# Two gated feed-forwards cut in parts of 6, 8 and 8 tiles, and wave tables made in the layers

## The chip, the cores and the metric

The kernel runs on one core of a Trainium2 chip. The metric is the device time of one execution in microseconds; lower is better. Five engines work side by side, each through its own list of instructions in order: TensorE (PE) multiplies, VectorE (DVE), ScalarE (ACT) and GpSimd (POOL) do elementwise work, and SyncE (SP) mostly issues transfers. They wait for each other by semaphores.

## The reference, cut to what matters

```python
D_MODEL, SEQ, DEPTH, D_FF_2 = 1024, 512, 2, 2816

def first_block(x, ...):                     # two layers
    for l in range(DEPTH):                   # attention, convolution, retention, and then
        ...                                  # x + rms_norm(square(relu(rms_norm(x) @ w_up)) @ w_down)

def swiglu_ffn(x, w_in, w_down):             # w_in 1024 x 5632, w_down 2816 x 1024
    a, b = jnp.split(x @ w_in, 2, axis=-1)
    return (jax.nn.silu(a) * b) @ w_down

def hybrid_layer_2(x, mem, ...):             # the third part
    x = x + 0.5 * swiglu_ffn(rmsnorm(x, ffn1_norm), ffn1_w_in, ffn1_w_down)
    u = rmsnorm(x, mix_norm)
    ...       # a scan with cos and sin of (a_im * dt) * t, attention, memory attention, w_out
    x = x + 0.5 * swiglu_ffn(rmsnorm(x, ffn2_norm), ffn2_w_in, ffn2_w_down)
    return x
```

`mem` (256 x 1024) is normalised too and multiplied by `w_kv` right after the first feed-forward. All of it is float32.

## The kernel before

Activations stand with features on the 128 partitions and the 512 tokens along a row, so 1024 features are 8 tiles. A float32 product is made of three matmuls of a faster type: each operand is split in a rounded part (`_hi`) and the rest (`_lo`), and hi*hi, hi*lo and lo*hi are added in PSUM. `product` does this for a block of weights of up to 1024 rows and 256 columns: 2 output tiles x 8 x 3 = 48 matmuls of 512 tokens. The weights come in blocks into `w_raw` (two slots). ScalarE copies a block to `w_hi` (`round_block`), VectorE subtracts to get `w_lo` (`rest_block`), both two blocks ahead of TensorE; SyncE issues the next load when the slot is free.

**Quarter products.** `seven` does a block of 1024 x 256 weights by Strassen's scheme: tokens, weight rows and weight columns are cut in halves, and seven products of quarters (each 4 x 3 matmuls of 256 tokens) take the place of eight. The price is on the other engines. `seven_sums` and `last_sum` make four sums of weight quarters, `pair_round` and `pair_rest` split the seven weight terms in four steps, and `one_product`, `two_products`, `three_products`, `last_late`, `last_early` and `first_late` put the outputs together from the four banks. The fifth product adds to the bank of the first, so TensorE waits until `one_product` (ScalarE, to `two_sum`) has copied it; the sixth waits for `three_products`. Before the first quarter product of a feed-forward `whole_scaled` (VectorE) makes the normalised activations `h_whole`, `direct_round` and `direct_rest` split them, `token_sums` (GpSimd) forms the sums of token halves in place, and `sums_round` (ScalarE) and `sums_rest` (VectorE) split these to `t_hi` and `t_lo`. TensorE waits on `whole` for all of it.

**The two layers.** A layer's feed-forward has four parts of 4 up blocks and 4 down blocks. The up blocks of part 0 are direct, those of parts 1 to 3 are quarter products. The code calls the four down blocks of a part `downs`, and `begun` is the first quarter block of the next part, whose weights are prepared beside the last two down blocks.

**The third part.** The second feed-forward (`ffn2`) is cut in parts of 8, 8 and 6 of its 22 tiles: up blocks of the part, then its four down blocks, which VectorE adds to `x_sb` with factor 0.5. Part 0 is direct and parts 1 and 2 (14 pairs of an `a` and a `b` tile) are quarter products. The first feed-forward (`ffn1`) is direct throughout: 11 turns of two up blocks, `g_hi` and `g_lo` with all 22 tiles, and then 16 down blocks (6, 6, 5 and 5 tiles for each of 4 output pairs), which add up in PSUM.

Beside these 16 blocks of `ffn1` stand two pieces of other work. One is the norm of `mem`. The other is the wave tables, cos and sin of the scan's phases, 16 of them, each 128 x 2 x 512: `whole_turns` (GpSimd, 2 instructions), `phase_step` (VectorE, 3), `waves` (ScalarE, 3), and a store to `trig_kept` in DRAM issued by SyncE. The buffer `made` holds three of them.

The order of all this is written out by hand, engine by engine: `layer_scalar`, `layer_vector` and `layer_gpsimd` for the layers, `third_scalar` and its like for the third part.

## Time and profile before

| | us |
|---|---|
| median of 3 runs | 2402.59 |
| lowest, highest | 2402.18, 2402.71 |
| the profiled execution | 2402.1 |
| its span in the trace | 2400.3 |
| TensorE busy | 2385.4 |
| VectorE busy | 1591.3 |
| ScalarE busy | 1094.6 |
| GpSimd busy | 344.6 |

The span goes from the first to the last instruction of the trace; 1.8 us of the execution's time lie around it. Busy times are sums of the instructions' times with overlaps counted once. A matmul's printed duration reaches beyond the start of the next one, so TensorE's pace is read from starts. A row in time order gives the start, the duration, the engine, the line of the kernel, the operation and `out<-in`; what stands in brackets is the idle time before it and who ended it.

### The profile page before, as it was taken

What the parts mean: (1) busy time and instruction counts of PE and PEld (TensorE: products, weight loads), DVE (VectorE), ACT (ScalarE), POOL (GpSimd) and SP (SyncE); (2) the same over time, 40 slices, a digit from 0 to 9 for tenths busy, and PEclk for the clock granted to TensorE, in tenths of its full rate; (3) what the DMA queues carried; (4) which work ended last, traced back from release to release, by engine and by line L of the source; (5) the groups of instructions that cost most, each with busy time, mean ns of one, the idle gap of its engine ahead of it and who ended that gap; (6) DMA issues with size and microseconds to landing.
All of it is one profiled execution on the core that took longest, in us unless ns stands there. A gap on an engine that the chain in (4) does not pass through costs nothing.

```text
span 2400.3 us, 33986 instructions
## 1 busy us (share of the span) xinstructions
PE 2385.4 (99%) x13482; PEld 2014.5 (84%) x13482; DVE 1591.3 (66%) x2231; ACT 1094.6 (46%) x1626; POOL 344.6 (14%) x259
## 2 busy tenths in 40 slices
PE   9999999999999999999999999999999999999998
PEld 7877998998886989889988888877778788889997
DVE  7775775665977567557644347769995386359685
ACT  5346553555445546336522236522335564335444
POOL 1231030001132121001111124300000121120001
PEclk9999999999999999999999999999999999999999
DMA  4312222323230222223232225643442143222322
GB/s 169 145 45 88 89 87 90 123 88 106 101 128 18 106 90 104 88 106 109 86 105 89 103 102 183 221 148 119 145 158 80 49 169 134 88 106 82 114 87 88
DMA packets 46849, 260.13 MB, mean 108 GB/s; under 512 B 5424, under 2 KB 7984, under 8 KB 22768
## 3 DMA queue, kind: packets, MB, share of 16 engines
q1 hardware_dynamic: 44448, 249.07, 29.6%
q0 software_dynamic: 640, 5.51, 0.6%
q10 hardware_dynamic: 1616, 3.54, 0.5%
q8 instruction: 101, 1.65, 0.3%
q14 instruction: 44, 0.36, 0.1%
HBM read 240.27 MB, written 16.78 MB: 107 GB/s over the span
## 4 chain that ended last, share of the span: by engine, by line
PE 91%; DVE 5%; ACT 2%; issue 2%; DMA 0%; DVEq 0%; SPq 0%; ACTq 0%
PE gemm L487 60%; PE gemm L1104 5%; PE gemm L1105 5%; PE gemm L1106 5%; PE gemm L780 1%; PE gemm L791 1%; PE gemm L782 1%; DVE w_lo L437 1%; DVE out_sb L1912 1%; PE turned L1418 1%; PE mixed L1432 1%; PE score L1409 1%; PE gemm L520 1%; PE gemm L673 1%; PE gemm L674 1%
## 5 line engine op out<-in xcount | busy, mean ns | idle before, releaser
L437 DVE TENSOR_TENSOR w_lo<-w_raw,w_hi 128x2048 fp32r<-128x2048 f32 (+4 forms) x157 | 341.9, 2177 | 204.9 <-ACT w_hi L429 204.8
L487 PE MATMUL gemm<-h_hi,w_hi 128*128 128x512 f32 x1136 | 454.2, 400 | 1.0 <-DVE w_lo L437 1.0
L487 PE MATMUL gemm<-h_hi,w_lo 128*128 128x512 f32 x1136 | 443.3, 390 | 0.0
L487 PE MATMUL gemm<-h_lo,w_hi 128*128 128x512 f32 x1136 | 442.7, 390 | 0.0
L429 ACT ACTIVATE w_hi<-w_raw 128x2048 fp32r<-128x2048 f32 (+4 forms) x167 | 292.9, 1754 | 202.9 <-PE gemm L487 169.0
L487 PEld LDWEIGHTS gemm<-h_hi,w_hi 128*128 128x128 f32 x1136 | 213.6, 188 | 55.5 <-issue 8.3
L487 PEld LDWEIGHTS gemm<-h_hi,w_lo 128*128 128x128 f32 x1136 | 213.2, 188 | 45.5
L487 PEld LDWEIGHTS gemm<-h_lo,w_hi 128*128 128x128 f32 x1136 | 213.6, 188 | 42.2 <-issue 1.0
L487 PE MATMUL gemm<-f_hi,w_hi 128*128 128x512 f32 x480 | 187.2, 390 | 0.7
L487 PE MATMUL gemm<-f_hi,w_lo 128*128 128x512 f32 x480 | 186.8, 389 | 0.0
L487 PE MATMUL gemm<-f_lo,w_hi 128*128 128x512 f32 x480 | 186.8, 389 | 0.0
L1104 PE MATMUL gemm<-t_hi,w_hi 128*128 128x256 f32 x608 | 172.3, 283 | 0.0
L1105 PE MATMUL gemm<-t_lo,w_hi 128*128 128x256 f32 x608 | 172.0, 283 | 0.0
L1106 PE MATMUL gemm<-t_hi,w_lo 128*128 128x256 f32 x608 | 172.0, 283 | 0.0
L1042 ACT ACTIVATE w_hi<-w_raw 128x1024 fp32r<-128x1024 f32 x76 | 80.5, 1059 | 169.7 <-DVE w_raw L1021 98.7
L487 PE MATMUL gemm<-g_hi,w_hi 128*128 128x512 f32 x340 | 132.5, 390 | 0.0
L487 PE MATMUL gemm<-g_lo,w_hi 128*128 128x512 f32 x340 | 132.3, 389 | 0.0
L487 PE MATMUL gemm<-g_hi,w_lo 128*128 128x512 f32 x340 | 132.3, 389 | 0.0
L1105 PE MATMUL gemm<-h_lo,w_hi 128*128 128x256 f32 x456 | 129.0, 283 | 0.0
L1106 PE MATMUL gemm<-h_hi,w_lo 128*128 128x256 f32 x456 | 129.0, 283 | 0.0
L1104 PE MATMUL gemm<-h_hi,w_hi 128*128 128x256 f32 x456 | 129.0, 283 | 0.0
L1051 DVE TENSOR_TENSOR w_lo<-w_raw,w_hi 128x1024 fp32r<-128x1024 f32 x76 | 93.9, 1236 | 37.5 <-ACT w_hi L1042 37.0
(549 smaller groups left out, 5315.9 us busy)
## 6 DMA issues: line engine op xcount, KB each, us to landing
w_raw<-in_w SPq DMA_DIRECT2D x179, 1024.0 KB, 4.8
w_raw<-in_w SPq DMA_DIRECT2D x12, 768.0 KB, 4.2
w_raw<-in_w SPq DMA_DIRECT2D x17, 512.0 KB, 3.8
trig_kept<-made SPq DMA_DIRECT2D x16, 512.0 KB, 5.9
trig<-trig_kept SPq DMA_DIRECT2D x16, 512.0 KB, 6.5
w_raw<-in_w SPq DMA_DIRECT2D x8, 640.0 KB, 4.5
bias_t<-in_att_bias SPq DMA_DIRECT2D x2, 1536.0 KB, 9.1
decay_t<-in_c_decay SPq DMA_DIRECT2D x2, 1536.0 KB, 8.0
```

The lines of the kernel that those rows point to most:

```text
L429: act.activation(flat(w_hi, b), flat(w_raw, b), ACT.Copy).then_inc(S["w_rounded"], 1)
L437: dve.tensor_tensor(flat(w_lo, b), flat(w_raw, b), flat(w_hi, b).bitcast(F32), ALU.subtract).then_inc(S["w_rest"], 1)
L487: mm = pe.matmul(dst, lhs, rhs, start=b.first and k == 0 and j == 0, stop=b.last and k == b.kt - 1 and j == 2)
L520: pe.matmul(dst, wh[:, k, c], hi[:, k, :], start=k == 0, stop=False)
L673: pe.matmul(dst, wh[:, k, c], h_hi[:, k, :], start=k == 0, stop=False)
L674: pe.matmul(dst, wl[:, k, c], h_hi[:, k, :], start=False, stop=False)
L780: pe.matmul(dst, wh[:, k, c], h_hi[:, k, TOKENS[e]], start=k == 0 and m == 0, stop=False, skip_group_check=True)
L1042: act.activation(pair_of(w_hi, b, q), pair_source(b, q), ACT.Copy).then_inc(S["term_hi"] if q < 3 else S["w_rounded"], 1)
L1051: dve.tensor_tensor(pair_of(w_lo, b, q), pair_source(b, q), pair_of(w_hi, b, q).bitcast(F32), ALU.subtract).then_inc(S["term_lo"] if q < 3 ...
L1104: pe.matmul(dst, wh[:, c], h, start=q < 4 and k == 0, stop=False, skip_group_check=q >= 4)
L1105: pe.matmul(dst, wh[:, c], r, start=False, stop=False, skip_group_check=q >= 4)
L1106: mm = pe.matmul(dst, wl[:, c], h, start=False, stop=k == 3, skip_group_check=q >= 4)
```

## The change

Both feed-forwards of the third part go through one function for each engine, with parts of 6, 8 and 8 tiles. Part 0 is direct, and the other 16 pairs are quarter products: 16 more in `ffn1` and 2 more in `ffn2`. The loops of `ffn1` are written out. The norm of `mem` moves into part 1 of `ffn1`, beside its down blocks.

The wave tables are made in the two layers. Each down block of parts 1 and 2 of a layer gets one wave, at its end in the code, so a layer makes 8 and both make 16. `made` holds one wave now, so `whole_turns` of a wave waits for the store of the wave before. The store is issued by ScalarE, right after the wave; after the fourth wave of a part `log_and_exp` loads ScalarE's table for the rest of the layer.

```diff
-FFN_PARTS = (6, 6, 5, 5)
-GATED_PARTS = (8, 8, 6)
+GATED_PARTS = (6, 8, 8)
...
-    ffn("ffn1")
+    def gated(name):
+        for part, tiles in enumerate(GATED_PARTS):
+            start[f"{name}_up{part}"] = len(out)
+            at = sum(GATED_PARTS[:part])
+            if part:
+                for t in range(at, at + tiles):
+                    out.append(Piece(0, t * P, WCOLS, KD, "seven", name + "_in"))
+            else:
...
+            for j in range(DM // WCOLS):
+                out.append(Piece(at * P, j * WCOLS, WCOLS, tiles, "feat", name + "_down"))
+
+    gated("ffn1")
...
             token_sums(pool, cnt)
             for part in range(1, PARTS):
-                for b in plan1[UP[part]:UP[part] + 4]:
+                for b in plan1[UP[part] + (part > 1):UP[part] + 4]:
                     last_sum(pool, b)
+                if part == 1:
+                    pool.wait_ge(S["units"], plan1[DOWN[1]].u0)
+                    pool.dma_start(time_t[:], A["c_time"]).then_inc(S["time_in"], 16)
...
+                if part < PARTS - 1:
+                    for j in range(4):
+                        whole_turns(pool, wave_at(lay, part, j))
+                        if j == 2:
+                            last_sum(pool, plan1[UP[part + 1]])
...
                     else:
                         for q in range(2) if j == 2 else range(2, 4):
                             pair_round(act, begun, q)
...
+                    if part:
+                        waves(act, wave_at(lay, part, j))
+                        if j == 3:
+                            log_and_exp(act)
...
                     else:
                         for q in range(2, 4):
                             pair_rest(dve, begun, q)
+                    if (lay, part, j) == (0, 0, 1):
+                        steps_and_turns(dve, step)
+                    if part:
+                        phases(dve, wave_at(lay, part, j))
...
-        made = at("made", [P, 3, 2, SEQ], F32, 66)
+        time_t = at("time_t", [P, SEQ], F32, FZ + 72)
+        made = at("made", [P, 2, SEQ], F32, FZ + 74)
...
+        def whole_turns(pool, s):
+
+            if s:
+                pool.wait_ge(*wave_stored(s - 1))
+            to = made[:, 0, :]
...
+        def waves(act, s):
+
+            act.wait_ge(S["phased"], s + 1)
...
+            act.dma_start(trig_kept[s], made[:]).then_inc(S[f"trig_moved{s % 3}"], 16)
...
+            for part in range(len(GATED_PARTS)):
+                if part:
+                    seven_part("ffn1", part)
+                ups, downs = gated_blocks("ffn1", part)
+                for j, b in enumerate(downs):
+                    def mem_total(m):
+                        if (part, j, m) == (1, 1, 1):
+                            pe.wait_ge(S["sq_added"], added_by(MEM_NORM))
...
+                    if (part, j) == (1, 1):
+                        mem_squares_added()
+                    if (part, j) == (1, 2):
+                        mem_scaled()
+                    down_rests("ffn1", part, j)
```

**ScalarE at the end of a layer's down blocks, part 1.** First before the change, from the weights of `begun` to `one_product` (`two_sum`) and on:

```order
L1042 ACTIVATE w_hi<-w_raw 128x1024 [waits w_in1,units]
L1042 ACTIVATE w_hi<-w_sums 128x512 [waits last_summed,units]
L1180 ACTIVATE two_sum<-gemm 128x256 [waits term_read]
L1042 ACTIVATE w_hi<-w_raw 128x1024 [waits w_summed,term_read]
L1042 ACTIVATE w_hi<-w_sums 128x1024 [waits w_summed,term_read]
```

The same place after the change:

```order
L1036 ACTIVATE w_hi<-w_raw 128x1024 [waits w_in1,units]
L1036 ACTIVATE w_hi<-w_sums 128x512 [waits last_summed,units]
L2355 ACTIVATE made<-made 128x512 [waits phased]
L2357 ACTIVATE made<-made 128x512 [waits trig_s]
L2358 ACTIVATE made<-made,quarter 128x512
L2360 DMA trig_kept<-made 128x1024 [waits trig_s]
L570 ACT_TABLE_LOAD
L1174 ACTIVATE two_sum<-gemm 128x256 [waits term_read]
L1036 ACTIVATE w_hi<-w_raw 128x1024 [waits w_summed,term_read]
L1036 ACTIVATE w_hi<-w_sums 128x1024 [waits w_summed,term_read]
```

The fourth wave, its store and a table load now stand between the weights of `begun` and the copy of its first product.

**VectorE at the same place.** Before, from the adding of the last two down blocks to `three_products`:

```order
L1051 TENSOR_TENSOR w_lo<-w_raw,w_hi 128x1024 [waits term_hi]
L1051 TENSOR_TENSOR w_lo<-w_sums,w_hi 128x1024 [waits term_hi]
L2109 TENSOR_TENSOR out_sb<-out_sb,gemm 128x512 [waits units,g_free]
L2109 TENSOR_TENSOR out_sb<-out_sb,gemm 128x512 [waits units]
L1051 TENSOR_TENSOR w_lo<-w_raw,w_hi 128x1024 [waits term_hi]
L1051 TENSOR_TENSOR w_lo<-w_sums,w_hi 128x512 [waits w_rounded]
L1118 TENSOR_TENSOR two_sum<-two_sum,gemm 128x256 [waits first_out,term_read]
L1018 TENSOR_TENSOR w_sums<-w_raw 128x512 [waits term_lo,w_in0]
```

After:

```order
L2386 SCALAR_TENSOR_TENSOR made<-time_t,state_par,made 128x512 [waits turns_s]
L2389 SCALAR_TENSOR_TENSOR made<-time_t,state_par,made 128x512 [waits fract]
L2392 TENSOR_SCALAR made<-made 128x512 [waits fract_low]
L2123 TENSOR_TENSOR out_sb<-out_sb,gemm 128x512 [waits units,g_free]
L2123 TENSOR_TENSOR out_sb<-out_sb,gemm 128x512 [waits units]
L1045 TENSOR_TENSOR w_lo<-w_raw,w_hi 128x1024 [waits term_hi]
L1045 TENSOR_TENSOR w_lo<-w_sums,w_hi 128x512 [waits w_rounded]
L2386 SCALAR_TENSOR_TENSOR made<-time_t,state_par,made 128x512 [waits turns_s]
L2389 SCALAR_TENSOR_TENSOR made<-time_t,state_par,made 128x512 [waits fract]
L2392 TENSOR_SCALAR made<-made 128x512 [waits fract_low]
L1112 TENSOR_TENSOR two_sum<-two_sum,gemm 128x256 [waits first_out,term_read]
L1012 TENSOR_TENSOR w_sums<-w_raw 128x512 [waits term_lo,w_in0]
```

The third wave stands ahead of the last two additions and the fourth ahead of `two_products`; each waits for GpSimd (`turns_s`).

**VectorE beside the down blocks of part 0 in `ffn2`.** Before:

```order
L1192 TENSOR_TENSOR h_lo<-h_whole,h_hi 128x2048 [waits more_hi]
L3731 SCALAR_TENSOR_TENSOR x_sb<-gemm,x_sb 128x512 [waits units] x2
L437 TENSOR_TENSOR w_lo<-w_raw,w_hi 128x2048 [waits w_rounded]
L3731 SCALAR_TENSOR_TENSOR x_sb<-gemm,x_sb 128x512 [waits units] x2
L437 TENSOR_TENSOR w_lo<-w_raw,w_hi 128x2048 [waits w_rounded]
L1198 TENSOR_TENSOR t_lo<-h_whole,t_hi 128x2048 [waits more_hi] x2
L3731 SCALAR_TENSOR_TENSOR x_sb<-gemm,x_sb 128x512 [waits units] x2
```

After:

```order
L1186 TENSOR_TENSOR h_lo<-h_whole,h_hi 128x2048 [waits more_hi]
L3367 SCALAR_TENSOR_TENSOR x_sb<-gemm,x_sb 128x512 [waits units] x2
L427 TENSOR_TENSOR w_lo<-w_raw,w_hi 128x1536 [waits w_rounded]
L3367 SCALAR_TENSOR_TENSOR x_sb<-gemm,x_sb 128x512 [waits units] x2
L427 TENSOR_TENSOR w_lo<-w_raw,w_hi 128x1536 [waits w_rounded]
L1192 TENSOR_TENSOR t_lo<-h_whole,t_hi 128x2048 [waits more_hi] x2
L3367 SCALAR_TENSOR_TENSOR x_sb<-gemm,x_sb 128x512 [waits units] x2
```

Nothing moved; the down blocks' weights are 6 tiles instead of 8. `ffn1` now has the same rows.

## Rows read from the trace of the kernel before

**Rows 1.** the page: TensorE (PE) busy, and its granted clock
```profile
PE 2385.4 (99%) x13482; PEld 2014.5 (84%) x13482; DVE 1591.3 (66%) x2231; ACT 1094.6 (46%) x1626; POOL 344.6 (14%) x259
...
PEclk9999999999999999999999999999999999999999
```

**Rows 2.** the waits of TensorE, whole span: total us, times, longest
```profile
PE mixed L725 <- DVE sq_f L917: 1.6, 2, 0.8
PE turned L1248 <- DVE rs L1359: 1.5, 1, 1.5
```

**Rows 3.** TensorE in time order: start us, duration, engine, line, operation
```profile
2128.43 0.39 PE L487 MATMUL gemm<-g_hi,w_hi 128*128 128x512 f32 x1
...
2171.95 0.28 PE L1104 MATMUL gemm<-h_hi,w_hi 128*128 128x256 f32 x1
```

**Rows 4.** busy time by window: eight pairs by quarter products, VectorE as DVE
```profile
2172.00:2252.00 80.00, 80.00 (x669) 80.00 (x668) 74.15 (x114) 44.47 (x63) 0.00 (x0) 1.00 0.30 107
```

**Rows 5.** VectorE, GpSimd, ScalarE before the first quarter products, in time order
```profile
2134.04 5.38 DVE L1184 SCALAR_TENSOR_TENSOR h_whole<-x_sb,par_sb,rs 128x512 f32<-128x512 f32 x8
...
2143.79 13.70 POOL L1152 TENSOR_TENSOR h_whole<-h_whole 128x1024 f32<-128x1024 f32 x4 [23.30 <-DVE h_lo L1192]
...
2157.52 3.72 ACT L1173 ACTIVATE t_hi<-h_whole 128x2048 fp32r<-128x2048 f32 x2 [5.14 <-POOL h_whole L1152]
...
2159.47 4.50 DVE L1198 TENSOR_TENSOR t_lo<-h_whole,t_hi 128x2048 fp32r<-128x2048 f32 x2 [4.24 <-ACT t_hi L1173]
...
2165.08 0.69 DVE L1018 TENSOR_TENSOR w_sums<-w_raw 128x512 f32<-128x512 f32 x1
...
2168.28 1.23 DVE L1051 TENSOR_TENSOR w_lo<-w_raw,w_hi 128x1024 fp32r<-128x1024 f32 x1 [0.46 <-ACT w_hi L1042]
...
1442.91 1.76 DVE L437 TENSOR_TENSOR w_lo<-w_raw,w_hi 128x1536 fp32r<-128x1536 f32 x1
```

**Rows 6.** the first layer, end of its second down projection, in time order
```profile
416.14 0.28 PE L1104 MATMUL gemm<-h_hi,w_hi 128*128 128x256 f32 x1
...
421.89 0.28 PE L1104 MATMUL gemm<-h_hi,w_hi 128*128 128x256 f32 x1
...
385.71 2.29 DVE L437 TENSOR_TENSOR w_lo<-w_raw,w_hi 128x2048 fp32r<-128x2048 f32 x1 [1.32 <-ACT w_hi L429]
...
410.46 1.21 DVE L1051 TENSOR_TENSOR w_lo<-w_sums,w_hi 128x1024 fp32r<-128x1024 f32 x1
...
418.58 0.69 DVE L1051 TENSOR_TENSOR w_lo<-w_sums,w_hi 128x512 fp32r<-128x512 f32 x1
...
421.48 0.41 DVE L1125 TENSOR_TENSOR three_sum<-two_sum,gemm 128x256 f32<-128x256 f32 x1
...
417.83 0.36 ACT L1180 ACTIVATE two_sum<-gemm 128x256 f32<-128x256 f32 x1
```

**Rows 7.** one wave in time order (POOL, DVE, ACT), and a table load
```profile
1469.82 0.70 POOL L2773 TENSOR_SCALAR made<-time_t,state_par 128x512 f32<-128x512 f32 x1 [3.60 <-DMA trig_kept<-made]
...
1472.13 0.75 DVE L3292 SCALAR_TENSOR_TENSOR made<-time_t,state_par,made 128x512 f32<-128x512 f32 x1 [2.21 <-POOL made L2776]
...
1474.17 0.63 ACT L2860 ACTIVATE made<-made 128x512 f32<-128x512 f32 x1 [1.37 <-DVE made L3301]
...
1475.37 0.71 ACT L2863 ACTIVATE made<-made,quarter 128x512 f32<-128x512 f32 x1
...
1430.19 1.28 ACT L2928 ACT_TABLE_LOAD   x1
```

**Rows 8.** the stores of the waves, issue to landing; transfers at 404 to 412
```profile
DMA to landing us min/median/max: 2.6/5.9/7.4
...
404.00:412.00 8.00, 8.00 (x37) 6.64 (x36) 5.32 (x7) 2.01 (x2) 1.29 (x1) 1.00 0.00 0
```

**Rows 9.** squares of the memory and their addition, in time order
```profile
1420.33 2.55 ACT L536 ACTIVATE mem_t<-mem_sb 128x256 f32<-128x256 f32 x8
...
1424.11 2.32 DVE L3355 TENSOR_TENSOR mem_t<-mem_t 128x1024 f32<-128x1024 f32 x2
```

More of the change, by code:

```diff
@@ L254, in third_pieces @@
         out.append(Piece(0, c, WCOLS, KD, "feat", "w_out2"))
[L255 to L267 removed]
+    gated("ffn2")
     return out, start
@@ L2368, in third_sync @@
         def third_sync(sp):
[L2369 to L2375 removed]
+            for b in plan2[0:AT2["u"]]:
                 load_block(sp, b)
[L2377 to L2379 removed]
             def load_trig(s):
@@ new lines, in third_tensor @@
+            opening_in_halves(pe, ups[:2], 2 * DEPTH - 1, sq_f)
+            for n, b in enumerate(ups[2:]):
+                product(pe, b, h_hi, h_lo, each=None if n else second_total(pe, 2 * DEPTH - 1, sq_f))
+            for part in range(len(GATED_PARTS)):
[6 more added lines that the diff above has]
+                            pe.wait_ge(S["sq_added"], added_by(MEM_NORM))
+                            pe.matmul(o_ps[:, 0:MEM], ones[:], mem_sq[:, 0, :], start=True,
+                                      stop=True).then_inc(S["norm_sum"], 1)
+                    product(pe, b, g2_hi, g2_lo, tile_ready=None if j else (S["g2_s"], sum(GATED_PARTS[:part])),
+                            halfway=mem_total)
@@ new lines, in seven_part @@
+            def seven_part(name, part):
+                ups, downs = gated_blocks(name, part)
+                for u, b in enumerate(ups):
+                    if u:
+                        pair_round(act, b, 3)
+                    one_product(act, b)
+                    if u:
+                        gated_round(ups[u - 1], u - 1)
+                    for q in range(3):
+                        if q == 2:
+                            gate_kept(b)
+                        if not b.closes:
+                            pair_round(act, plan[b.n + 1], q)
+                        elif q < 2:
+                            begun_round(act, downs[0], q)
+                    gate_silu(b)
+                gated_round(ups[-1], len(ups) - 1)
+                round_block(act, downs[1].n)
@@ new lines, in down_rounds @@
+            def down_rounds(name, part, j):
+                ups, downs = gated_blocks(name, part)
+                if part == 0 and j == 0:
+                    direct_round(act, gated_counts(name), ups[-1])
+                if part == 0 and j == 2:
+                    sums_round(act, gated_counts(name))
+                if j < 2 or part == LAST_PART:
+                    round_block(act, downs[j].n + 2)
+                else:
+                    begun = gated_blocks(name, part + 1)[0][0]
+                    for q in range(2) if j == 2 else range(2, 4):
+                        pair_round(act, begun, q)
@@ L2945, in third_scalar @@
+            norm_squares(act, x_sb, x2_sq, wait=(S["g_free"], downs[0].t0), tiles=(KD - 2, KD - 1))
             norm_rooted(act, N0 + 2)
@@ L3238, in third_scalar @@
+                if part < LAST_PART:
+                    for j, b in enumerate(downs):
+                        down_rounds("ffn2", part, j)
             log_and_exp(act)
```

702 lines of the change are left out of this document (289 added, 413 removed).

## The prediction

> **What bounds the kernel now.** I read four views in this order. The page says how full TensorE is: it is busy for 99% of the span, and its granted clock never shows less than 9 tenths [rows 1]. The waits of TensorE say that nothing stands in front of it: no wait of the whole span is over 1.5 us [rows 2], and in a stretch of quarter products TensorE is busy 80 of 80 us [rows 4]. So matmuls taken out shorten the span one for one, and any wait that is put in front of TensorE lengthens it one for one. The order in time then gives TensorE's pace, and the last view is the same stretch on the other engines, to see how close they run behind it.
>
> Pace. In the second feed-forward of the third part, the down products of part 0 (4 blocks of 48 matmuls, 192 in all) start at 2128.43 and the first quarter product starts at 2171.95 [rows 3]: 43.52 us / 192 = 0.2267 us for a matmul of 512 columns. In the quarter products 669 matmuls of 256 columns take 80.00 us [rows 4]: 0.120 us each. The durations printed for one matmul overlap and are not used.
>
> **What the matmuls save.** A direct pair of tiles is 2 tiles x 8 x 3 = 48 matmuls: 48 x 0.2267 = 10.88 us. A pair by quarter products is 7 x 4 x 3 = 84: 84 x 0.120 = 10.08 us. The gain is 0.80 us a pair. The first feed-forward changes 16 pairs, the second 2 more than before (14 to 16): 18 x 0.80 = 14.4 us. The down products keep their matmuls (22 x 8 x 3 in either cut). In the steady part of the eight pairs VectorE is busy 74.15 of 80 us [rows 4], and TensorE has no wait. The first feed-forward runs the same instructions on each engine, so I cost its steady part at nothing; the cover is those 6 us, 0.7 us a pair.
>
> The Trainium skill (TensorE: Matmul & The Clock Gate, Part 1) gives start-to-start as N / 2.4 GHz plus 2.5 ns. An estimate from that page is 215.8 and 109.2 ns, 1.19 us a pair and 21 us in all. The rows disagree with it for these matmuls, more so at 256 columns, and the measurement decides.
>
> **Entry to the quarter products: part 0 has 6 tiles in place of 8.** Before the first quarter product, the whole normalised activations have to be made, summed by GpSimd, rounded by ScalarE and subtracted by VectorE. This chain starts when the last up product ends and is covered by the down products of part 0. Counted from 2128.43 [rows 3, 5]: VectorE starts h_whole at +5.6, GpSimd's sums run from +15.4 to +29.1 (13.70 us), ScalarE rounds t_hi from +29.1, VectorE's t_lo runs +31.0 to +35.5, the weight sums start at +36.7, and the first w_lo of the quarter products ends at 2169.51, +41.1. The down products end at +43.5: 2.4 us to spare. After the change the down products are 144 matmuls, 144 x 0.2267 = 32.6 us. The chain keeps every step. Only the weights ahead of it are smaller: VectorE's 128x1536 takes 1.76 us where 128x2048 takes 2.29 [rows 5, 6], and ScalarE's copy ahead of it shrinks in a like share, by my estimate 0.4 us. So w_lo is ready at +40.2 and TensorE waits 7.6 us. Bounds: 5 us (a chain shorter by the 2.3 us that t_lo's second half takes, if less traffic speeds the shared engines) and 8.5 us (no shortening). I take 7.6, since every row of the chain is this kernel's. Both feed-forwards enter this way: 2 x 7.6 = 15.2 us, of which nothing was paid before.
>
> **The waves in the layers.** Each layer has two down stretches (its parts 1 and 2) of four blocks of 10.9 us, and each block now gets one wave: GpSimd 2 instructions, VectorE 3, ScalarE 3 and a store issued by ScalarE. One buffer holds the wave, so GpSimd may begin wave s only when the store of wave s-1 has landed. Costs by the old waves [rows 7]: GpSimd 1469.82 to 1472.13, 2.3 us; VectorE to 1474.17, 2.0; ScalarE to 1476.08, 1.9. The store took 2.6 to 7.4 us, median 5.9, there in competition with weight loads; here the queues are idle (share 0.00 from 404 to 412 [rows 8]), so I take 3.0 with its issue. For the first three waves of a stretch VectorE and ScalarE have idle time, and their place is late in the block, so they are hidden. The fourth is not. Follow the first layer [rows 6]: VectorE ends the second w_lo at 411.67, and wave 2 is next: VectorE 413.6, ScalarE 415.6, store landed 418.6, GpSimd 420.9 for wave 3, VectorE 422.9, ScalarE 424.9, issue of the store and then a table load of 1.28 [rows 7]: 426.4. Only then, in ScalarE's order, comes the copy two_sum, 0.36 us: 426.8. It started at 417.83 before. TensorE's fifth quarter product adds to the bank that this copy reads, and started at 421.89. It now waits 5.0 us. VectorE then has the addition after the copy, three weight sums and three_sum, whose end the sixth product wants: about 2.75 us after the copy (421.48 + 0.41 minus the end of the weights at 419.2), against 1.44 us of the fifth product, so 1.3 us more. The next block starts with VectorE about a microsecond later than usual, and I add 0.1. The sum is 6.4 us a stretch, 4 stretches: 25.6 us. Queued behind VectorE's wait for wave 3 are exactly those additions; behind ScalarE's, the copy and the next weights' rounding; behind GpSimd's, one weight sum. Bounds: if wave 3's turns are ready when VectorE gets there (419.3), the copy ends at 424.8 and the loss is 4.2 us. With stores of 5.9 us each, waves 1 and 2 slip too, the copy ends near 431.7, and the loss is 11.4 us. I take 6.4, as the store's row is nearest the short end when nothing competes.
>
> In the first feed-forward the 16 waves go away from VectorE, ScalarE, GpSimd and SyncE's queue, which also loses 16 stores and their waits. They lay beside matmuls there and TensorE had no wait, so this gains nothing. GpSimd's one weight sum a stretch that now stands behind wave 2 ends near 415.3, ahead of ScalarE's use of it at 417.3.
>
> **The memory's norm.** It now stands in part 1 of the first feed-forward. ScalarE has, after block 0 (10.9 us), the weight copy (about 1.9), a table load 1.28 and eight squares 2.55 [rows 7, 9]; VectorE adds them in 2.32 and about 0.7: 20.2 us after the start of the down products. TensorE wants the sum halfway through the second tile of block 1: 16.3 + 2.7 = 19.0. I cost it at 1.1 us, between 0 and 2.
>
> **Sum.** -14.4 + 15.2 + 25.6 + 1.1 = +27.5 us. The profiled run took 2402.1 us, 0.5 below the median of 2402.59, so I add the sum to the median: 2430 us.
>
> **Rivals.** Chances are at the end of each.
> (1) The forecast, all four terms: 2430 us. 0.40.
> (2) The same waits, and the clock falls in them. No row shows TensorE idle for more than 1.5 us [rows 2] and the clock is full throughout [rows 1], so a pause of 5 to 8 us is new here. If the first two quarter products after an entry (24 x 0.120 = 2.9 us) ran at half pace, 2.9 us more twice, and about 0.6 in each layer stretch, where half is hidden by the wait for three_sum: 8 us, 2438. The Trainium skill (TensorE: Matmul & The Clock Gate, Part 1) says that an idle array drops to half clock and recovers with activity; no row here shows it. 0.22.
> (3) Stores at their old median: 25.6 becomes 45.6, 2450 us. Against it is the idle share [rows 8]. 0.06.
> (4) Only the entries wait, since the layers' waves finish in time: 2404.5 us. It needs a chain 5 us shorter than the rows. 0.09.
> (5) Only the layers wait: 2415 us. 0.10.
> (6) The other side: cover holds, and TensorE is never last in any of the six places. The one mechanism is that GpSimd, whose steps head both chains, runs faster beside a less busy VectorE. It decides from a mean wait of 2.4 us at each of six places (14.4 / 6). All waits gone gives 2388 us. For it: old GpSimd steps overlapped VectorE's. Against: GpSimd is 13.7 of 41 us at the entry and 2.3 of 15 in the layers; it would have to be twice as fast, and the order in ScalarE's queue stays. 0.13.
>
> **How the numbers follow.** The likeliest is 2430. About 0.2% (5 us) is what a measurement of this kernel tells from no change. Faster: case 6, 0.13. Same: case 4, 0.09, and a little of 5: 0.10. Slower: the rest, 0.77. The range leaves out case 6 and most of case 3: 2404 to 2446. It takes in the entry waits at 5 to 8.5, the layers at 4.2 up to 9, and the clock.
>
> **What would show it.** In the waits of TensorE: two of 7 to 8 us for VectorE's w_lo at the entries of the feed-forwards, four of about 5 us in the layers for ScalarE's two_sum, each followed by about 1.3 us for three_sum, and one of a microsecond for the memory's sum. The steady quarter products of the first feed-forward should keep 0.120 us. The granted clock after the waits decides case 2. If the fourth wave's VectorE steps stand ahead of 419 us in the first layer, my store or GpSimd price is wrong; if t_lo ends before +30, the entry is.

## The result: slower by 2.0%, and by 20 us more than forecast

| | before | after |
|---|---|---|
| median, us | 2402.39 (4 runs) | 2449.85 (4 runs) |
| lowest, highest | 2402.05, 2402.71 | 2448.48, 2450.84 |
| ratio, 95% interval | | 1.0197 (1.0183 to 1.0210) |
| span of the profiled execution | 2400.3 | 2449.0 |
| TensorE's mean granted clock | 0.999 | 0.989 |

The kernel lost 47.5 us where 27.5 was forecast, outside the range of 2404 to 2446. These are the waits of TensorE after the change; before it, no wait was over 1.5 us [rows 2]. Columns: who waited for whom, us in total, times, longest.

```profile
PE gemm L1098 <- ACT two_sum L1174: 25.3, 4, 6.6
PE gemm L1098 <- issue: 8.1, 2, 4.0
PE mixed L554 <- DVE x_sq L623: 4.8, 1, 4.8
PE gemm L477 <- DVE w_lo L427: 4.7, 4, 2.0
```

Row 1 is the four layer stretches (a stretch is the four quarter blocks behind a part's down blocks) and row 2 the two entries. Row 3 is the end of `ffn1`. Row 4 is mostly the down blocks of part 0 in both feed-forwards, 1.98 and 1.97 us. The forecast had no wait over a microsecond in the places of rows 3 and 4.

**The first of the four stretches, in the first layer.** This is the place of [rows 6], in time order on VectorE, ScalarE, GpSimd and TensorE. Waves are numbered from 0 within a part, so wave 3 is the fourth. L2386 to L2392 are VectorE's steps of a wave, L2355 to L2358 ScalarE's, L2335 and L2338 GpSimd's.

```profile
412.69 0.74 DVE L2386 SCALAR_TENSOR_TENSOR made<-time_t,state_par,made 128x512 f32<-128x512 f32 x1
...
422.17 0.75 DVE L2386 SCALAR_TENSOR_TENSOR made<-time_t,state_par,made 128x512 f32<-128x512 f32 x1 [2.17 <-POOL made L2338]
```
```profile
416.65 0.33 ACTq L2360 DMA_DIRECT2D trig_kept<-made  x1
...
424.21 0.63 ACT L2355 ACTIVATE made<-made 128x512 f32<-128x512 f32 x1 [5.55 <-DVE made L2392]
...
426.50 1.28 ACT L570 ACT_TABLE_LOAD   x1 [0.39 <-ACT made L2358]
427.79 0.38 ACT L1174 ACTIVATE two_sum<-gemm 128x256 f32<-128x256 f32 x1
```
```profile
419.32 1.24 POOL L2335 TENSOR_SCALAR made<-time_t,state_par 128x512 f32<-128x512 f32 x1 [8.77 <-DMA trig_kept<-made]
420.65 1.49 POOL L2338 TENSOR_SCALAR made<-made 128x512 f32<-128x512 f32 x1
```
```profile
428.32 0.55 PE L1098 MATMUL gemm<-h_hi,w_hi 128*128 128x256 f32 x1 [5.59 <-ACT two_sum L1174]
```

Wave 2 starts on VectorE at 412.69, its store is issued at 416.65 and landed at 419.3, GpSimd ends wave 3's turns at 422.1, and the copy `two_sum`, which stood at 417.83 before [rows 6], starts at 427.79. TensorE idles 5.59 us.

**The clock after it.** The same stretch in windows. A row gives the window, its length, the busy time (and the number of instructions) of PE, PEld, DVE, ACT and POOL, then PEclk, the granted clock, and the share and GB/s of the transfers.

```profile
422.40:428.40 6.00, 0.41 (x4) 0.24 (x3) 1.83 (x4) 3.54 (x5) 0.00 (x0) 0.93 0.53 220
428.40:434.00 5.60, 5.60 (x26) 5.51 (x27) 5.14 (x8) 2.29 (x4) 1.28 (x1) 0.50 0.00 0
434.00:436.00 2.00, 2.00 (x17) 2.00 (x17) 1.47 (x3) 1.97 (x3) 0.00 (x0) 0.89 0.00 0
```

From 427.6, still within the wait, the granted clock is 0.50, the 1.2 GHz level, until about 434.4. Matmuls of 256 columns start 0.213 us apart there, and 0.120 us apart before and after.

**An entry**, in `ffn1`. The down products of part 0 start at 1273.65; two waits of TensorE follow, with VectorE's first `w_lo` of them, its `t_lo`, and GpSimd's sums:

```profile
1292.11 0.50 PE L477 MATMUL gemm<-g_hi,w_hi 128*128 128x512 f32 x1 [1.98 <-DVE w_lo L427]
...
1312.76 0.55 PE L1098 MATMUL gemm<-h_hi,w_hi 128*128 128x256 f32 x1 [4.03 <-issue]
```
```profile
1289.08 2.98 DVE L427 TENSOR_TENSOR w_lo<-w_raw,w_hi 128x1536 fp32r<-128x1536 f32 x1
...
1302.63 4.49 DVE L1192 TENSOR_TENSOR t_lo<-h_whole,t_hi 128x2048 fp32r<-128x2048 f32 x2 [6.71 <-ACT t_hi L1167]
```
```profile
1288.04 12.61 POOL L1146 TENSOR_TENSOR h_whole<-h_whole 128x1024 f32<-128x1024 f32 x4 [22.34 <-DVE h_lo L1186]
```

The view names no engine for the second wait (`issue`). The first `w_lo` of quarters ends at 1312.65, 0.11 us ahead of the matmul, so I put the wait down to it. That is +39.0 on the forecast's scale (+40.2 there, +41.1 before). The six-tile down products take 1312.76 - 1273.65 = 39.11 us in place of 144 x 0.2267 = 32.65: 6.46 of wait, 1.98 of it in the middle and 4.03 at the end. Behind the second the clock is down again:

```profile
1309.00:1313.00 4.00, 0.24 (x1) 0.27 (x2) 3.48 (x5) 2.65 (x3) 0.00 (x0) 0.83 0.00 0
1313.00:1315.00 2.00, 2.00 (x10) 2.00 (x11) 2.00 (x4) 0.82 (x2) 0.00 (x0) 0.50 0.00 0
...
1319.00:1321.00 2.00, 2.00 (x19) 2.00 (x19) 1.91 (x4) 0.30 (x1) 0.00 (x0) 1.00 0.87 356
```

**The end of `ffn1`.** ScalarE, GpSimd and TensorE at the squares of x for the next norm:

```profile
1565.05 1.91 ACT L419 ACTIVATE w_hi<-w_raw 128x2048 fp32r<-128x2048 f32 x1 [7.93 <-PE gemm L477]
1566.87 2.17 ACT L526 ACTIVATE x_sq<-x_sb 128x512 f32<-128x512 f32 x4
```
```profile
1567.56 4.25 POOL L546 TENSOR_TENSOR x_sq<-x_sq 128x512 f32<-128x512 f32 x2 [6.56 <-ACT x_sq L526]
```
```profile
1572.66 2.08 PE L554 MATMUL mixed<-x_sq,fixed 128*128 128x512 f32 x2 [4.84 <-DVE x_sq L623]
```

ScalarE's rounding of weights waits until the last down block is done, and the squares of four tiles stand behind it; GpSimd's last two additions behind those. Nothing of these steps is covered by products.

**The ledger**, from starts of matmuls in both traces (the first row from their pace):

| place | forecast | measured |
|---|---|---|
| 18 pairs by quarter products | -14.4 | -14.4 |
| four layer stretches, 49.39 + 49.48 + 49.76 + 50.01 against 40.61 each | +25.6 | +36.2 |
| two entries: waits 2 x 6.46, then 83.21 and 82.93 for eight pairs against 80.63 | +15.2 | +17.8 |
| memory's norm (down products of part 1: 44.53 against 43.55) | +1.1 | +1.0 |
| end of the last down product of `ffn1` to the products of u: 32.33 against 25.44 | 0 | +6.9 |
| sum | +27.5 | +47.5 |

The difference of the medians is 47.5 too, but the two profiled executions differ by 48.7. The 1.2 us that no row has are 0.7 ahead of the layers' first product and a wait of 0.8 us for ScalarE's `spare_bc` in the middle of the third part, less small differences. So the sum meets the medians only to about a microsecond. Not all of the memory's 1.0 is new either: see below.

### The profile page after: what moved, and what is told of

Its sections match the earlier page's. It is cut to its first block, busy times and chain, and to the rows that moved or that the text cites. A ratio compares the mean times of both kernels' runs of the same rounds, so it can differ in the third digit from the quotient of the medians.

```text
span 2449.0 us, 35468 instructions
## 1 busy us (share of the span) xinstructions
PE 2391.3 (98%) x14142; PEld 2048.8 (84%) x14142; DVE 1711.6 (70%) x2455; ACT 1157.9 (47%) x1726; POOL 341.7 (14%) x246
## 4 chain that ended last, share of the span: by engine, by line
PE 85%; DVE 7%; ACT 4%; issue 2%; DMA 1%; POOL 1%; ACTq 0%; DVEq 0%; SPq 0%; POOLq 0%
PE gemm L477 48%; PE gemm L1098 7%; PE gemm L1099 7%; PE gemm L1100 7%; PE gemm L770 1%; PE gemm L781 1%; PE gemm L772 1%; DVE w_lo L427 1%; DVE w_lo L1045 1%; DVE out_sb L1926 1%; PE turned L1412 1%; PE mixed L1426 1%; ACT w_hi L419 1%; PE score L1403 1%; PE gemm L510 1%
## 5 line engine op out<-in xcount | busy, mean ns | idle before, releaser
L427 DVE TENSOR_TENSOR w_lo<-w_raw,w_hi 128x2048 fp32r<-128x2048 f32 (+3 forms) x133 | 295.5, 2222 | 165.2 <-ACT w_hi L419 165.1
L477 PE MATMUL gemm<-h_hi,w_hi 128*128 128x512 f32 x848 | 342.3, 404 | 1.5 <-ACT spare_bc L3086 0.8
L419 ACT ACTIVATE w_hi<-w_raw 128x2048 fp32r<-128x2048 f32 (+3 forms) x143 | 252.7, 1767 | 176.6 <-PE gemm L477 142.1
L477 PE MATMUL gemm<-h_hi,w_lo 128*128 128x512 f32 x848 | 331.3, 391 | 0.0
L477 PE MATMUL gemm<-h_lo,w_hi 128*128 128x512 f32 x848 | 330.6, 390 | 0.0
L1098 PE MATMUL gemm<-t_hi,w_hi 128*128 128x256 f32 x896 | 257.4, 287 | 0.5 <-DVE three_sum L1119 0.2
L1099 PE MATMUL gemm<-t_lo,w_hi 128*128 128x256 f32 x896 | 255.8, 286 | 0.0
L1098 PEld LDWEIGHTS gemm<-t_hi,w_hi 128*128 128x128 f32 x896 | 174.6, 195 | 1.9 <-DVE three_sum L1119 1.3
L1099 PEld LDWEIGHTS gemm<-t_lo,w_hi 128*128 128x128 f32 x896 | 174.5, 195 | 0.0
L1100 PEld LDWEIGHTS gemm<-t_hi,w_lo 128*128 128x128 f32 x896 | 174.3, 195 | 0.0
```

Of the source, the lines that this page charges most:

```text
L419: act.activation(flat(w_hi, b), flat(w_raw, b), ACT.Copy).then_inc(S["w_rounded"], 1)
L427: dve.tensor_tensor(flat(w_lo, b), flat(w_raw, b), flat(w_hi, b).bitcast(F32), ALU.subtract).then_inc(S["w_rest"], 1)
L477: mm = pe.matmul(dst, lhs, rhs, start=b.first and k == 0 and j == 0, stop=b.last and k == b.kt - 1 and j == 2)
L1098: pe.matmul(dst, wh[:, c], h, start=q < 4 and k == 0, stop=False, skip_group_check=q >= 4)
L1099: pe.matmul(dst, wh[:, c], r, start=False, stop=False, skip_group_check=q >= 4)
L1100: mm = pe.matmul(dst, wl[:, c], h, start=False, stop=k == 3, skip_group_check=q >= 4)
```

## The experiments

My theory at this point: in each place TensorE waits for a step that stands behind too much in its engine's order, and behind each wait the half clock costs extra, some 1.75 us a stretch and 2.5 an entry. The rival was that the clock costs nothing, or that GpSimd's or VectorE's load, not the order, is the cause. All are edits of the changed kernel (2449.85) unless told.

**Parts of 8, 8, 6**

```diff
-GATED_PARTS = (6, 8, 8)
+GATED_PARTS = (8, 8, 6)
```

> The changed kernel with both feed-forwards of the third part cut in 8, 8, 6 tiles instead of 6, 8, 8. Part 0 has four blocks of 64 down products again in place of 48, and each feed-forward has 14 pairs by quarter products in place of 16. Theory (the two entries cost what the trace of the changed kernel shows: 6.46 us each of waits in the down blocks of part 0, and about 2.5 us each afterwards at half clock): the 4 pairs that go back to direct products cost 4 x 0.80 = 3.2 us, 2 x 8.9 = 17.8 us come back, so 14.6 us less than the changed kernel, near 2435 us, with no wait of TensorE over 1.5 us at either entry, and the first quarter products after it at full clock. Rival (the slow clock there has another reason than the pause, as the start of quarter products itself): only 2 x 6.46 = 12.9 us come back, 9.7 us less in all, 2440 us, and the granted clock after the entry is still 0.5.

2434.26 us, 15.6 less. There is no wait over 0.6 us at the entries, and the eight pairs of part 1 take 80.63 us in both feed-forwards. The granted clock no longer falls there. The entries' whole loss hangs on six-tile part 0, the half clock included.

**The fourth wave in the second quarter block**, at the end of its turn in `layer_scalar`, and the like with `phases` in `layer_vector`:

```diff
...
+                        if part > 1 and b is run[1]:
+                            waves(act, wave_at(lay, part - 1, 3))
+                            log_and_exp(act)
```

> The changed kernel with one edit in the layers: VectorE's, and ScalarE's, steps of the fourth wave of a down stretch (and ScalarE's table load behind them) stand at the end of the second block of quarter products that follows, instead of ahead of the copy two_sum. Nothing else moves. Theory (the whole loss of the layers, 36.2 us over four stretches, hangs on ScalarE's copy standing behind the fourth wave): the stretches take 40.6 us again, and the time falls by 33 to 36 us, to 2414 to 2417 us; the clock stays full there. Rival A (part of the loss is GpSimd's: its steps of the waves slow VectorE in the whole stretch, whatever stands in the fourth place): 10 us or less come back. Rival B (the fourth wave is only late somewhere else, where the quarter products have VectorE close to its limit of 6 us in 80): 20 to 30 us come back and a new wait of 1 to 3 us stands in the second or third block.

2441.77 us, only 8.1 less: a miss. The stretches take 47.22, 48.15, 48.49 and 48.29 us, 6.5 less together. The rest, 1.6 us, is about what the two entries gave, which nothing edited: the eight pairs behind them take 82.19 us each, for 83.21 and 82.93. The wait moved by two blocks (TensorE, first layer):

```profile
445.18 0.36 PE L1098 MATMUL gemm<-h_hi,w_hi 128*128 128x256 f32 x1 [3.02 <-ACT two_sum L1174]
```

ScalarE there, from the wave to the next copy:

```profile
439.36 0.63 ACT L2358 ACTIVATE made<-made 128x512 f32<-128x512 f32 x1 [1.08 <-DVE made L2395]
...
441.66 1.28 ACT L570 ACT_TABLE_LOAD   x1 [0.39 <-ACT made L2361]
442.95 0.63 ACT L1036 ACTIVATE w_hi<-w_sums 128x512 fp32r<-128x512 f32 x1
...
444.67 0.37 ACT L1174 ACTIVATE two_sum<-gemm 128x256 f32<-128x256 f32 x1
```

So the fourth wave is not only late for one copy. In a quarter block the chain from VectorE to ScalarE to TensorE has no room for 2.0 us of VectorE and, behind it, 3.6 us of ScalarE, though ScalarE is busy less than half of the time. My rival B was the right kind, but I had sized it at 20 to 30 us back; it was 8.

**Squares of x ahead of the rounding**

```diff
+                    if part == LAST_PART and j > 1:
+                        k = 2 * j - 4
+                        norm_squares(act, x_sb, x2_sq, wait=(S["g_free"], downs[0].t0), tiles=(k, k + 1))
+                        if j == 3:
+                            norm_squares(act, x_sb, x2_sq, wait=(S["g_free"], downs[0].t0), tiles=(4, 5))
                     down_rounds("ffn1", part, j)
...
-                    if part == LAST_PART and j:
-                        k = 2 * j - 2
-                        norm_squares(act, x_sb, x2_sq, wait=(S["g_free"], downs[0].t0), tiles=(k, k + 1))
```

> The changed kernel with one edit at the end of the first feed-forward: ScalarE squares the tiles 0 to 5 of x ahead of its rounding of the weights for later blocks, not behind it. Theory (the wait of 4.84 us for x_sq comes from ScalarE's squares of tiles 4 and 5, which stand behind the last rounding, and the products right after it run at half clock for about 1.1 us more): 5 us less than the changed kernel, 2445 us, and the wait is back at 0.4 us. Rival (the roundings become late instead, as they now stand behind the squares' waits for VectorE): the wait moves to TensorE's own down blocks, and the time stays within 1.5 us of the changed kernel.

2445.75 us, 4.1 less. The wait for `x_sq` is 2.12 us, not the 0.4 that I expected, and the end of `ffn1` takes 28.77 us in place of 32.33. What is left stood in the order too (tiles 6 and 7 behind the last rounding, VectorE's addition behind its last `w_lo`).

**TensorE kept busy in the waits**

```diff
                 if q == 4:
+                    if b.opens and b.n < DEPTH * n1 and b.run % 3:
+                        keep_clock(pe, s_ps[0][:], h_hi[:, 0, 0:P], h_hi[:, 0, :], 24)
                     pe.wait_ge(S["first_out"], 2 * b.count + 1)
...
                 if part == 1:
+                    keep_clock(pe, s_ps[0][:], g2_hi[:, 0, 0:P], g2_hi[:, 0, :], 18)
                     pe.wait_ge(S["whole"], gated_counts(name)("whole", KD + 4))
```

> The changed kernel with idle time of TensorE filled by products that nothing reads: 24 of 512 columns into a spare bank ahead of the fifth quarter product in the four layer stretches (the waits are 5.6 to 6.6 us), and 18 ahead of the wait at each of the two entries (4.0 us). ScalarE, VectorE and GpSimd do the same work at the same times, so no wait ends earlier. Theory (the pause lets the clock fall to half, and that costs time after it, 1.75 us a stretch and 2.5 us an entry): the clock stays above 0.9 there, and the time falls by about 4 x 1.75 + 2 x 2.5 = 12 us, at least by 6 if the filler at half clock runs over the end of the wait. Rival (the clock falls for another reason, or its fall is hidden behind VectorE and ScalarE, which are late there anyway): no change or a little more time, 2449 to 2453 us, and the matmuls after the fillers still have a pitch of 213 ns.

2447.55 us, 2.3 less. The granted clock is 1.00 in the windows of both places (after the entry, and behind the fillers in the layer):

```profile
1313.00:1317.00 4.00, 4.00 (x36) 4.00 (x35) 4.00 (x7) 0.39 (x1) 0.00 (x0) 1.00 0.20 25
```
```profile
430.00:432.00 2.00, 1.34 (x11) 1.34 (x12) 1.57 (x4) 1.63 (x2) 1.29 (x1) 1.00 0.00 0
```

At the entries that brings 2.0 and 1.8 us: the eight pairs take 81.19 and 81.17 where they took 83.21 and 82.93. The fillers themselves cost nothing there (39.11 us from the first down product to the first quarter product, as without them). In the layers it brings 0.6 us in the first stretch and nothing in the other three (49.51, 49.78, 49.84 against 49.48, 49.76, 50.01), because the faster matmuls run into the next wait:

```profile
430.66 0.39 PE L1100 MATMUL gemm<-t_hi,w_hi 128*128 128x256 f32 x1 [1.09 <-DVE three_sum L1121]
```

VectorE can do its additions and sums only once the copy is there. Whether TensorE runs at half pace or waits a second time is the same. The half clock was real in all six places and cost time in three, the two entries and, little, the first stretch: 4.4 us by the traces. The medians differ by 2.3, less than they can tell surely, as the two kernels' runs overlap (2446.28 to 2449.25 against 2448.48 to 2450.84). It is not the 12 that I expected.

**No table load behind the fourth wave**

```diff
                         waves(act, wave_at(lay, part, j))
-                        if j == 3:
-                            log_and_exp(act)
```

> The changed kernel without the table load that ScalarE does behind the fourth wave of each down stretch; the table is loaded where the next norm wants it. Theory (the copy two_sum is late by the whole chain ahead of it, and whatever is taken off ScalarE's end of the chain comes back): 1.28 us a stretch come back, 4 x 1.28 = 5.1 us; behind the second stretch of each layer the load comes back on the path of the norm, 2 x 1.28 = 2.6 us. Together 2.5 us less than the changed kernel, 2447 us, and TensorE's four waits are 4.3 to 5.3 us in place of 5.6 to 6.6. Rival (the half clock behind the wait costs time of its own, and a shorter wait keeps the clock up): 5 us or more less.

2451.11 us where I expected 2447. That is 1.3 more, within the spread of the runs (2449.23 to 2453.24), and the two profiled executions are equal (2450.95 and 2450.84). The four waits fell to 4.3 to 5.3 us as expected and the stretches gave back 6.2 us (47.72, 47.66, 48.48, 48.56), but as much came back in more places than I had counted. The waits of TensorE that are new or longer:

```profile
PE gemm L477 <- DVE w_lo L427: 5.5, 6, 2.0
...
PE gemm L770 <- ACT h_hi L838: 3.8, 4, 1.3
...
PE gemm L477 <- DVE swi L3401: 1.0, 1, 1.0
```

3.8 + 1.0, another 1.0 for `ca` and 0.8 more for `w_lo` are 6.6 us, against the 6.2 given back. The row of `h_hi` is the norm, which is done in halves: four waits in two layers, where I had counted one a layer.

**A buffer of its own for GpSimd's turns**

```diff
+        turned_t = at("turned_t", [P, SEQ], F32, FZ + 78)
...
-                pool.wait_ge(*wave_stored(s - 1))
-            to = made[:, 0, :]
+                pool.wait_ge(S["fract"], s)
+            to = turned_t[:]
...
+            if s:
+                dve.wait_ge(*wave_stored(s - 1))
```

> The changed kernel with a buffer of 2 KB a partition of their own for GpSimd's turns. GpSimd then waits for VectorE's read of the wave before, and no longer for its store; VectorE waits for the store. Theory (the chain store, GpSimd, VectorE, ScalarE sets the end of the copy, as in my replay): GpSimd's two steps, 2.8 us from 419.3 to 422.1 in the first layer, leave the chain, and the copy ends 2.8 us earlier in each of four stretches: 11 us less than the changed kernel, 2439 us. Rival (the shared path of VectorE and GpSimd, or the place of the copy behind ScalarE's other work, sets it): 4 us less or nothing.

2435.96 us, 13.9 less. The stretches take 47.92, 46.22, 46.49 and 46.66: 11.3 less, as expected, though 1.5 in the first and 3.3 in the others. Of the other 2.6 us, 1.7 lie at the entries, which nothing edited: the eight pairs take 81.99 and 82.40. VectorE now has the fourth wave right behind its weights, and only the order remains:

```profile
419.57 0.74 DVE L2389 SCALAR_TENSOR_TENSOR made<-time_t,state_par,turned_t 128x512 f32<-128x512 f32 x1
```
```profile
423.89 1.28 ACT L570 ACT_TABLE_LOAD   x1 [0.39 <-ACT made L2359]
425.18 0.38 ACT L1174 ACTIVATE two_sum<-gemm 128x256 f32<-128x256 f32 x1
```

**Each wave at the start of its block**: `phases` in `layer_vector`, `last_sum` in `layer_gpsimd`, and in `layer_scalar`, not printed, `waves` with the table load ahead of `round_block` and `pair_round` (the calls at the blocks' ends are gone):

```diff
+                        phases(dve, wave_at(lay, part, j))
                         added_down(b, part)
...
-                        if j == 2:
+                        if j == 3:
                             last_sum(pool, plan1[UP[part + 1]])
```

> The changed kernel with each wave at the start of its down block in place of its end, on VectorE (ahead of the addition added_down) and on ScalarE (ahead of the rounding), and GpSimd's one weight sum behind the fourth wave. The same work, the same buffer. By the durations seen so far a wave goes round in 9.5 to 10 us (GpSimd 2.9, VectorE 2.0, ScalarE 2.0, store 2.6 to 3), so the fourth ends about 40 us after the start of the down products, ahead of their end at 43.5. Theory (the order in the queues is all: the fourth wave stands ahead of the copy two_sum and ends after it is wanted): TensorE's four waits go, the stretches take 40.6 to 41 us, and the time falls by 34 to 36 us, to 2414 to 2416 us. Rival A (there is no room for the fourth wave's 2.0 us of VectorE and 3.3 us of ScalarE with its table load between the last down block and the third quarter product, as the version with the fourth wave in the quarter products suggests): 8 to 20 us come back, with waits of 2 to 4 us in the same places. Rival B (waves ahead of the additions delay the down blocks' own weights): new waits for w_lo of 1 to 2 us in the down blocks.

2427.06 us, 22.8 less: between theory and rival A. The stretches take 42.78, 44.37, 44.95 and 44.37. The fourth wave still holds up ScalarE, whose rounding starts 2.65 us behind the first quarter product, for 0.20 before, as it stands behind the table load:

```profile
417.82 1.28 ACT L570 ACT_TABLE_LOAD   x1 [0.39 <-ACT made L2357]
419.12 1.06 ACT L1036 ACTIVATE w_hi<-w_raw 128x1024 fp32r<-128x1024 f32 x1
```

TensorE now waits for VectorE, which follows ScalarE's rounding and copy. The largest row, beside 3.2 us for its `w_lo`:

```profile
PE gemm L1098 <- DVE three_sum L1119: 6.6, 9, 1.5
```

Rival B's waits did not come: those for the down blocks' `w_lo` are 5.4 us in all, for 4.7.

With parts of 8, 8, 6 and the squares first in the same kernel:

> Three edits together: the waves at the start of their blocks, parts of 8, 8, 6 tiles in both feed-forwards, and ScalarE's squares of x ahead of the roundings at the end of the first feed-forward. Theory (the losses are separate and add up): the changed kernel's 2449.9 less 15.6 (parts, measured) less 4.1 (squares, measured) less 34 to 36 (waves): 2394 to 2396 us, 7 to 8 us below the kernel before, with no wait over 2.2 us on TensorE. If the waves give back only 8 to 20 us, 2410 to 2422 us.

2410.72 us, 39.1 less. As the waves gave back 22.8 and not 34 to 36, this is the second case of the expectation. The gains of the three single edits are 22.8 + 15.6 + 4.1 = 42.5, 3.4 more. Some 1.8 of that is counted twice: with the waves first the eight pairs behind the entries took 82.19 us each, 1.0 and 0.7 less than in the changed kernel, and parts of 8, 8, 6 take away that loss whole. One kernel's runs spread by 2 to 4 us. The places are nearly separate.

**The fourth wave one block sooner**, on top of the waves at the start of their blocks and the turns' own buffer, with parts of 6, 8, 8 (the edit beyond these two):

```diff
                         if part:
                             seven_sums(dve, begun)
+                            phases(dve, wave_at(lay, part, 3))
...
+                    if part and j == 2:
+                        waves(act, wave_at(lay, part, 3))
+                        log_and_exp(act)
```

> The version with the waves at the start of their down blocks, and two more edits: GpSimd's turns in a buffer of their own, and the fourth wave one block sooner (VectorE right behind the weight sums of the third down block and ahead of pair_rest, ScalarE behind the same block's two pair_round). Working from the trace of that version, first layer: VectorE's sums end at 408.4, the store of wave 2 has landed at 409.2, so VectorE has the fourth wave at 411.2, ScalarE 413.2, table load 414.5, and its next rounding can start at 416.6 as in the kernel before. Theory (only order and the chain through the one buffer made the layers wait, there is room for all the work): the stretches of quarter products take 40.6 to 41.2 us, 34 to 36 us less than the changed kernel in all, 2414 to 2416 us. Rival (VectorE's second and third weight steps, moved back by 2 us, become late for the fourth block's end or the first quarter product): 0.5 to 2 us of new wait a stretch, 2417 to 2424 us.

2414.01 us, 35.8 less. The stretches take 40.89, 40.60, 40.88 and 40.61, and the row for `two_sum` is gone from the waits. ScalarE in the first layer, third down block and after:

```profile
411.38 0.63 ACT L2358 ACTIVATE made<-made 128x512 f32<-128x512 f32 x1 [0.76 <-DVE made L2397]
...
413.68 1.28 ACT L570 ACT_TABLE_LOAD   x1 [0.39 <-ACT made L2361]
416.77 1.06 ACT L1036 ACTIVATE w_hi<-w_raw 128x1024 fp32r<-128x1024 f32 x1 [1.81 <-PE gemm L477]
...
418.25 0.36 ACT L1174 ACTIVATE two_sum<-gemm 128x256 f32<-128x256 f32 x1
```

Every wave is still made beside the same down blocks by the same instructions. So neither the amount of work nor GpSimd's and VectorE's slowing of each other was enough by itself to make the layers wait; the order and the one buffer were needed: 35.7 of the 36.2 us are back.

**All together**: the waves as in the last version, parts of 8, 8, 6, the squares of x ahead of each rounding and VectorE's addition ahead of its last `w_lo`:

> The same order of waves with parts of 8, 8, 6 tiles in both feed-forwards, and at the end of the first feed-forward ScalarE's squares ahead of each rounding (tiles 0 and 1 ahead of the second, 2 and 3 ahead of the third, 4 to 7 ahead of the fourth) and VectorE's one addition of squares ahead of its last w_lo. Theory (the losses are separate): 2449.9 less 15.6 (parts) less 34 to 36 (waves) less 5 to 6.5 (squares): 2392 to 2395 us, 7 to 10 us below the kernel before. Rival (a loss that was hidden behind another one shows now): 2396 to 2402 us.

2391.77 us (2391.58 to 2392.09), ratio to before 0.9956 (0.9942 to 0.9969). That is below both kernels and just under the 2392 to 2395 expected. Its waits are those of before:

```profile
PE mixed L715 <- DVE sq_f L907: 1.5, 2, 0.8
PE turned L1242 <- DVE rs L1353: 1.5, 1, 1.5
PE gemm L477 <- DVE w_lo L427: 1.1, 3, 0.6
```

With 14 pairs more by quarter products than before, the forecast's 0.80 us a pair gives 11.2 us; measured are 10.75. The end of `ffn1` takes 24.74 us against 25.44 before.

## Why the prediction was wrong

Of the 20.0 us between forecast and result, 10.6 are the layers' term (25.6, measured 36.2), 6.9 a place to which the sum gave nothing, and 2.6 the entries' term (15.2, measured 17.8). The layers' term alone brings the forecast to 2441, within the range; it takes the end of `ffn1` too to leave it.

**Right.** The saving: 0.80 us a pair, and quarter products at 0.120 us in `ffn1` too. The replay of the layer's chain: the copy's end was forecast for 426.8 us, and came at 428.17 in a trace that runs 0.7 later there. The stores: 2.6 us, near the 3.0 that I took and not the 5.9 of rival 3. The entry's chain: `w_lo` at +39.0 against +40.2.

**Right by luck: the memory's norm**, 1.0 against 1.1. The terms as they stand in the forecast (10.9, 1.9, 1.28, 2.55, 2.32, 0.7) add up to 19.65 and not to 20.2, so they give 0.65. The sum came at +19.4, and TensorE lost 0.4 us to it by starts. The rest of the 1.0 are the two products that use the sum (0.35) and a slower start behind them (0.2), which the kernel before had too, at another place (0.24 and 0.2).

**Wrong by size: the layers**, 9.05 us a stretch where I had 6.4. From the version with the full clock, where waits and pace are apart, in the first stretch: 5.7 us for the copy (I had 5.0), 1.25 for `three_sum` (1.3), and then 0.44 and 0.31 in the second and fourth block and 0.5 in slower starts around the waits, for which I had 0.1 in all. That is 8.2 us, and the half clock makes it 8.8. The sign of 1.3 us for `three_sum` did not show as a wait in the changed kernel (0.2 us in all), since TensorE at half clock came no sooner. In the other three stretches the first wait is 6.58, a microsecond more. There GpSimd's weight sum meets VectorE's second `w_lo` and both take longer, so wave 2 starts later (the second stretch; the other two read the same, 2.24 and 2.31, 2.23 and 2.31):

```profile
503.49 2.23 POOL L1022 TENSOR_TENSOR w_sums<-w_raw 128x512 f32<-128x512 f32 x1
```
```profile
504.49 2.31 DVE L1045 TENSOR_TENSOR w_lo<-w_sums,w_hi 128x1024 fp32r<-128x1024 f32 x1
```

In the stretch that I had followed they take 1.29 and 1.21 and do not overlap. The forecast had this weight sum end near 415.3, behind `w_lo` and harmless. I took one stretch for four.

**Wrong by size: the entries**, 8.9 us each where I had 7.6. The waits were 6.46, with the chain 1.2 us shorter than forecast and within my bounds, nearly all of it in GpSimd's sums (12.61 us for 13.70). The eight pairs behind them took 2.3 to 2.6 us more, of which keeping the clock up brought back 1.8 to 2.0. I had looked only at the end of part 0. The down blocks before it wait too (1.98 us), since `whole_scaled` and the splits stand ahead of their weights on VectorE and its `w_lo` takes 2.98 us beside GpSimd's sums, for 1.76. By the rows that cost nothing by itself: the chain to the first quarter `w_lo` does not pass through TensorE's down products, and TensorE would have waited that long at the end.

**Wrong in kind: the clock.** I put it as rival 2 and left it out of the sum. The granted clock fell to 0.50 at each of the seven waits of 4.0 us and more, and came back to 1.00 afterwards. The Trainium skill (TensorE: Matmul & The Clock Gate, Part 1) says that an idle array falls to half clock and recovers with activity. The rows at all seven agree. But its price cannot be read from the slower pitch, since it depends on who is late next: about 1.9 us at each entry, where TensorE alone sets the pace, some 1.1 at the end of `ffn1` (72 products take 10.14 us for 9.03), and 0.6, 0, 0 and 0 in the layers. My rival priced it at 2.9 an entry and 0.6 a stretch, 8 us in all, and had nothing for the end of `ffn1`: right that the entries pay more, too high by half for them.

**Missing: the end of `ffn1`**, 6.9 us. The forecast went through the code of the memory's norm and not through the other norm beside the down blocks. Before, ScalarE squared tiles 4 and 5 ahead of a rounding, 12 us before the down products ended at 1530.89:

```profile
1518.73 1.14 ACT L536 ACTIVATE x_sq<-x_sb 128x512 f32<-128x512 f32 x2
```

Only tiles 6 and 7 were left for later (1532.97), and TensorE waited 0.4 us. After, tiles 4 to 7 are squared at 1566.87, 2.1 us behind the end of the down products at 1564.79, and with GpSimd's two additions and the half clock behind the wait they lie on the path. The step that failed here is the sum's claim that its four terms were all: a loop was written anew, and I costed only what had moved in it. Moving squares and additions forward brought the place back to 24.74 us, for 32.33.

## What to carry to other kernels

Where TensorE is busy 99% of the time, the time of a change is found by asking for every place with a hand-over what each engine's order puts ahead of it, and by following each repeat of a pattern, not one. An engine that is busy half of the time can still have no room: 2.0 us of VectorE and 3.6 of ScalarE in a quarter block cost 6.6 to 7.9 us a stretch, and in the third down block, with the turns in their own buffer, 0 to 0.3. A single buffer between three engines and a store made a round of 9.5 us out of work of 7, and 2 KB more took a third of the layers' loss away.

## What the runs showed of the hardware

In the changed kernel, after the pauses of 4.0 to 6.6 us the granted clock was 0.50 and matmuls of 256 columns came 0.213 us apart, for 3.0 to 6.1 us. A pause of 1.98 us had no fixed effect: with the same wait in the same place the clock stayed at 1.00 in the changed kernel and fell in the version with the waves first, and the entry's total was the same (39.11 and 39.08 us), as the later wait took it up (4.03 and 2.38 us). Behind that later wait the eight pairs took 83.21 and 82.19 us with the same instructions, so the price of a fall in clock is good to about a microsecond from one version to another. Windows of the changed kernel, and of that version:

```profile
1292.00:1296.00 4.00, 3.89 (x17) 3.23 (x18) 3.92 (x4) 0.00 (x0) 3.92 (x2) 1.00 0.70 250
```
```profile
1270.00:1274.00 4.00, 4.00 (x13) 3.12 (x12) 3.38 (x3) 0.00 (x0) 3.92 (x2) 0.59 0.79 262
```

In the version with the waves first, GpSimd's first turn of a wave took 2.58 us where it began behind the start of VectorE's `w_lo` (398.12 to 400.41), and 0.70 where it began 0.36 us ahead of one:

```profile
398.40 2.58 POOL L2334 TENSOR_SCALAR made<-time_t,state_par 128x512 f32<-128x512 f32 x1 [6.67 <-DMA trig_kept<-made]
...
409.24 0.70 POOL L2334 TENSOR_SCALAR made<-time_t,state_par 128x512 f32<-128x512 f32 x1 [6.68 <-DMA trig_kept<-made]
```
